# A two-block model on one core: in the first mixer the turns of the input powers, the splits between scan units, the gate's sigmoids and the rows' load change places

## The reference, cut to what matters

```python
def s5_mixer(x, w_in, ..., d_skip, w_glu, b_glu, w_out):
    u, z = jnp.split(x @ w_in, 2, axis=-1)               # 2048 -> 2 x 1024
    ...                                                  # ar, ai: decay; bbar, c: input and output matrices
    _, _, h_r, h_i = lax.associative_scan(...)           # states, 64 groups x 64
    y = einsum(c_re, h_r) - einsum(c_im, h_i) + d_skip * u
    g = jax.nn.gelu(y)
    y = g * jax.nn.sigmoid(g @ w_glu + b_glu)
    return (y * jax.nn.silu(z)) @ w_out                  # 1024 -> 2048
```

## Time and profile before

| | |
|---|---|
| Median of three runs | 3044.75 us |
| Profiled execution, its own time | 3048.8 us |
| Its span in the trace | 3047.0 us |
| Granted clock, mean over the span | 0.991 |
| TensorE busy | 2974.8 us (98%) |
| VectorE busy | 2090.3 us (69%) |
| ScalarE busy | 1713.6 us (56%) |

### The profile page before, as it was taken

The page is one execution under the profiler, slowest core; times in us unless marked ns, Lnnn a source line. Parts: engine busy times, 40 slices in busy tenths (PEclk is TensorE's granted clock), DMA queues, the critical chain, the costliest instruction groups (busy, mean ns, idle before and its releaser), DMA issues.

```text
span 3047.0 us, 57764 instructions
## 1 busy us (share of the span) xinstructions
PE 2974.8 (98%) x23714; PEld 2469.0 (81%) x23714; DVE 2090.3 (69%) x2892; ACT 1713.6 (56%) x2261; POOL 151.1 (5%) x144
## 2 busy tenths in 40 slices
PE   7989999999999899999999999999999999999998
PEld 6868999999998799988999897777777777777654
DVE  7766445555666775756599997777777777777655
ACT  6544344666645533635545794445665656566676
POOL 6000000000000210000000350000000000000000
PEclk9999999999999999999999999999999999999999
DMA  6346565544473433535655426555656666656554
GB/s 231 92 171 211 173 189 177 148 151 147 138 248 114 132 125 113 165 118 182 207 174 189 150 95 220 191 198 189 201 188 199 194 201 194 200 188 206 195 199 152
DMA packets 143961, 529.78 MB, mean 174 GB/s; under 512 B 16992, under 2 KB 17760, under 8 KB 142048
## 3 DMA queue, kind: packets, MB, share of 16 engines
q1 hardware_dynamic: 141120, 515.57, 52.6%
q10 hardware_dynamic: 2592, 10.68, 1.0%
HBM read 521.99 MB, written 4.19 MB: 173 GB/s over the span
## 4 chain that ended last, share of the span: by engine, by line
PE 88%; DVE 6%; ACT 3%; DMA 2%; issue 1%; ACTq 0%; DVEq 0%; SPq 0%
PE ps L309 31%; PE ps L2912 22%; PE ps L2839 22%; DMA mem<-weights 2%; PE ps L451 1%; DVE mem L281 1%; PE ps L942 1%; PE ps L2884 1%; PE ps L1364 1%; PE ps L1991 1%; PE ps L1396 1%; ACT rounded L274 1%; PE ps L344 1%; PE ps L1977 1%; ACT mem L3000 0%
## 5 line engine op out<-in xcount | busy, mean ns | idle before, releaser
L281 DVE TENSOR_TENSOR mem<-mem,rounded 128x1024 bf16<-128x1024 f32 x940 | 1143.2, 1227 | 701.1 <-ACT rounded L274 689.5
L274 ACT CAST rounded<-mem 128x1024 fp32r<-128x1024 f32 x940 | 980.8, 1047 | 915.2 <-PE ps L309 287.4
L309 PE MATMUL ps<-rounded 128*128 128x256 f32 x3168 | 446.7, 290 | 17.5 <-DVE mem L281 17.5
L309 PEld LDWEIGHTS ps<-rounded 128*128 128x128 f32 x3168 | 397.1, 191 | 21.3 <-issue 16.2
L309 PE MATMUL ps<-mem,rounded 128*128 128x256 bf16 x3168 | 403.4, 274 | 1.4 <-DVE mem L281 1.4
L2912 PE MATMUL ps<-rounded 128*128 128x512 f32 x1024 | 337.0, 442 | 2.2 <-DVE mem L3309 2.0
L309 PEld LDWEIGHTS ps<-mem,rounded 128*128 128x128 bf16 x3168 | 302.2, 98 | 43.1 <-DVE mem L281 1.5
L2912 PE MATMUL ps<-mem,rounded 128*128 128x512 bf16 x1024 | 308.2, 383 | 0.0
L3010 ACT CAST mem<-mem 128x1024 bf16<-128x1024 f32 x204 | 213.6, 1047 | 155.5 <-PE ps L2912 68.4
L3299 DVE TENSOR_TENSOR mem<-mem,ps 128x512 f32<-128x512 f32 x384 | 263.1, 685 | 50.6 <-PE ps L2912 33.0
L2839 PE MATMUL ps<-rounded 128*128 128x256 f32 x2048 | 285.7, 287 | 0.5 <-ACT mem L3000 0.4
(11 more groups left out here) (447 smaller groups left out, 2973.7 us busy)
## 6 DMA issues: line engine op xcount, KB each, us to landing
mem<-experts SPq DMA_DIRECT2D x512, 512.0 KB, 4.0
mem<-weights SPq DMA_DIRECT2D x440, 512.0 KB, 3.7
mem<-x_t SPq DMA_DIRECT2D x4, 512.0 KB, 9.8
mem<-x_rows SPq DMA_DIRECT2D x1, 2048.0 KB, 8.4
mem<-cmp_w_k ACTq DMA_DIRECT2D x4, 512.0 KB, 5.0
mem<-cmp_w_v ACTq DMA_DIRECT2D x4, 512.0 KB, 5.2
h_rows<-mem SPq DMA_DIRECT2D x1, 2048.0 KB, 9.7
mem<-h_rows ACTq DMA_DIRECT2D x1, 2048.0 KB, 8.7
```

The costliest lines, as they stand in the source:

```text
L274: self.nc.scalar.copy(self.parts(r % SLOTS)[0], self.raw(r % RAW)).then_inc(self.high_done, with_skipped(c))
L281: self.nc.vector.tensor_tensor(wl, self.raw(r % RAW), wh.bitcast(F32), ALU.subtract).then_inc(self.low_done, with_skipped(c))
L309: mm = self.nc.tensor.matmul(self.ps[:, bank, half * 256:half * 256 + 256], a, b, start=(part == 0 and n == 0), stop=(part == PIECES - 1 a ...
```

## The change

The order changes at five places; no operation is added or dropped.
- TURN_AFTER: the four turns stand behind pieces 13, 16, 19 and 23, before behind 10, 13, 17 and 20. TURNED_AT and EXPAND_AT stay.
- VectorE: three low parts stand between the units (0,1) and (1,0), before four; three behind (1,1), before two. The product of z and the first half of gelu stands ahead of the low part of gelu's second half. Three, and then one, stand behind the two halves of the gated product, before two and two.
- ScalarE: two and three casts stand behind the two halves of gelu, before three and four. One follows the first sigmoids, and two stand before the second, as before.
- SP: pieces 42 and 43 are issued ahead of the rows of x, before behind them.

```diff
--- before.py
+++ after.py
@@ -632,7 +632,7 @@
 S5_GLOW, S5_YLOW, S5_SZ = S5_BT + 4096, S5_BT + 5120, S5_BT + 6144
 
 
-TURN_AFTER = (10, 13, 17, 20)
+TURN_AFTER = (13, 16, 19, 23)
 EXPAND_AT = (13, 15, 20, 24, 25, 27, 29)
 TURNED_AT = (17, 21, 26, 28)
 
@@ -721,7 +721,7 @@
                 sp.dma_start(k.raw(n), ins["weights"][n]).then_inc(k.landed[n], 16)
                 k.issued += 1
         k.stream(sp, AT_GLU, ahead=2 * RAW)
-        k.stream(sp, AT_A_OUT, ahead=2)
+        k.stream(sp, AT_A_OUT, ahead=PIECES)
         sp.wait_ge(h_ready, 4)
         sp.dma_start(rows, ins["x_rows"]).then_inc(xs, 16)
         k.stream(sp, AT_KV, ahead=0)
@@ -841,9 +841,10 @@
                 nc.scalar.activation(dst, src, ACT.Gelu_apprx_tanh).then_inc(gelu_done, 1)
             act.wait_ge(gelu_done, 2 * h + 2)
             nc.scalar.copy(half(gel_parts[0], h), half(gel, h)).then_inc(g_high, 1)
-            more(3 if h == 0 else 4)
+            more(2 if h == 0 else 3)
         for n in range(N_GLU):
-            more(2 * n)
+            if n:
+                more(2)
             t = AT_GLU + n
             act.wait_ge(k.multiplied, G0 + 6 + 2 * n)
             for sub in range(4):
@@ -852,6 +853,8 @@
                                             ps[:, t % BANKS + 3 * (sub // 2), (sub % 2) * T:(sub % 2) * T + T],
                                            ACT.Sigmoid, bias=small[:, 8 + j:9 + j])
                 last.then_inc(k.bank_free if sub == 3 else sig_done, 1)
+            if n == 0:
+                more(1)
             act.wait_ge(y_done, n + 1)
             nc.scalar.copy(half(yy_parts[0], n), half(yy, n)).then_inc(y_high, 1)
             act.dma_start(k.at((LN_G, LN_B)[n], 2048), ins[("ln_g", "ln_b")[n]][0]).then_inc(rows_in, 16)
@@ -1179,24 +1182,24 @@
 
         unit(0, 0)
         unit(0, 1)
-        more(4)
+        more(3)
         unit(1, 0)
         gel_low(0)
         unit(1, 1)
-        more(2)
+        more(3)
+        dve.wait_ge(z_done, 1)
+        v(tt(half(sz, 0), half(sz, 0), half(gel, 0), ALU.mult))
         gel_low(1)
         more(2)
-        dve.wait_ge(z_done, 1)
-        for h in range(2):
-            v(tt(half(sz, h), half(sz, h), half(gel, h), ALU.mult))
-            more(1)
+        v(tt(half(sz, 1), half(sz, 1), half(gel, 1), ALU.mult))
+        more(1)
         for h in range(2):
             dve.wait_ge(sig_done, 3 * h + 3)
             dve.wait_ge(k.bank_free, AT_GLU + h + 1 + BANKS)
             tt(half(yy, h), half(sig, h), half(sz, h), ALU.mult).then_inc(y_done, 1)
             dve.wait_ge(y_high, h + 1)
             tt(half(yy_parts[1], h), half(yy, h), half(yy_parts[0], h).bitcast(F32), ALU.subtract).then_inc(y_low, 1)
-            more(2)
+            more(3 if h == 0 else 1)
         dve.wait_ge(xs, 16)
         for n in range(N_A_OUT - 1):
             t = AT_A_OUT + n
```

## The result

| | median, us | ratio to before, 95% interval | profiled span, us |
|---|---|---|---|
| before | 3045.15 (5 runs) | | 3047.0 |
| changed | 3027.32 (5 runs, 3023.45 to 3033.69) | 0.9943 [0.9927, 0.9958] | 3025.5 |

What follows compares the result with a forecast made beforehand. The prediction took TensorE, 88% of the chain, as the bound, losing time to gaps and cold starts. Terms 12.0 + 3.8 + 8.0 give 23.8 us: 3048.8 profiled becomes 3025.0, or 3021 against the median; range 3017 to 3034.

Steps and rivals of the forecast that it cites:

- Part 1, the turns: Input-power turns on TensorE placed behind later pieces: no new waits, scans start earlier, 12.0 us gained.
- The third copy-out: ScalarE's copy-out before the fourth turn: ends at 85.9, turn at 86.9, the tightest place, clear by 1.0 us.
- The ceiling of 25.5 us: Most any ordering could give in the mixer: TensorE gaps of 18.2 us plus 7.3 us of slow clock.
- Part 2, the splits: Fewer VectorE splits between scan units: the 3.57 us gap before outputs (1,0) goes, 3.8 us gained.
- The wait for unit (1,1): TensorE's wait before outputs (1,1): grows from 0.69 to 2.0 us.
- Part 3, the sigmoids: Sigmoids ahead of casts on ScalarE: the 6.74 us wait and cold start before the output tiles go, 8.0 us gained.
- the table load: Sigmoid table load on ScalarE, 1.28 us: runs in the pause without a wait; if it waits, gain 22.5 us.
- Part 4, the rows' load: 2 MB load on SP's queue issued behind pieces 42 and 43: costs nothing, range 0 to about 4 us.
- main case: Whole kernel at 3019 to 3026 us, chance 0.64.
- rival A: Late landings starve three tight hand-overs, one gap again brings a cold start: gain 14 to 18, 3029 us, chance 0.17.
- a clock drop behind the wait for unit (1,1): Outputs (1,1) on TensorE might take 5.20 instead of 3.73 us, gain then 22.3 us; held 3 in 10.
- Rival D: Turns drain TensorE's stock of pieces, four times 8, 32 us lost against 23.8 gained: 3053 us, chance 0.04.

Runs made afterwards that it cites:

- run 11: Changed kernel with the fourth turn behind piece 21 instead of 23: median 3026.91 us, ratio 0.9942.
- run 12: Changed kernel with the four turns behind pieces 16, 19, 22 and 25: median 3037.43 us, ratio 0.9974.
- run 8: Changed kernel with four splits between units (0,1) and (1,0) and two behind (1,1), as before the change: 3027.39 us, ratio 0.9939.
- run 1: The changed kernel a second time, no edit: median 3025.16 us, ratio 0.9929.
- run 6: Changed kernel with casts 41 and 42 ahead of the first sigmoids, one ahead of the second, rows' load ahead of piece 42 again: 3034.04 us, ratio 0.9963.
- run 5: Changed kernel with casts 41 and 42 ahead of the first sigmoids, one cast ahead of the second: 3027.05 us, ratio 0.9938.
- run 7: Changed kernel with only the rows' load put back ahead of piece 42: 3025.56 us, ratio 0.9934.
- run 9: Changed kernel with two splits behind each gated half instead of three and one: 3023.18 us, ratio 0.9928.
- run 10: Changed kernel with two splits behind each gated half and the convolution's kernel products behind piece 28, not ahead of the first sums: 3021.43 us, ratio 0.9918.
- run 4: Changed kernel with two casts ahead of each of the two sigmoids: median 3037.71 us, ratio 0.9964.
- run 2: Kernel before with only the turns moved, behind pieces 13, 16, 19 and 23: median 3037.19 us, ratio 0.9968.

## Why the prediction was right

- **Part 1, the turns, 12.0 us.** Right. Undone alone they cost 9.7 (23.4 less 13.7), made alone they give 11.2. The third copy-out ended at 86.1 where 85.9 was worked out. The room ahead of the fourth turn was larger than the 1.0 us of the prediction, since the turn needs only the first copy: about 2.4 us, an estimate (87.18 less 84.05 and the 0.73 of run 11). Runs 11 and 12 show both sides of the place: the fourth turn two pieces earlier loses 3.4 us, all four three pieces later 13.9.
- **The ceiling of 25.5 us** was low by about 1.2: it counted the slow clock on the two turns and not on the pieces behind them (49.36 to 62.18 is 12.8 us, where a turn and three pieces take 10.0; from the fourth turn to the kernels 22.7, where 20.9 would do). Its two turn gaps with their cold starts make only 10.6, and its own steps gave 12.0.
- **Part 2, the splits, 3.8 us.** Right in place. Run 8 loses 4.8 us at the mixer's end, 1.6 of it by a clock drop, and that drop stood one wait later than forecast. The wait for unit (1,1) is 1.1 us (run 1), not 2.0.
- **Part 3, the sigmoids, 8.0 us: the sum right, its owner wrong.** With both edits undone the loss is 7.3 us (run 6), or 8.1 counted from outputs (1,1). The step that before "they stood behind casts 41 and 42, the latter waiting 5.34 us for its transfer" took that transfer as given. It was so late because of the rows' load, which the same change moves. With the load behind piece 43 the casts ahead of the sigmoids cost 2.4 us (run 5), the table load and a clock drop included.
- **Part 4, the rows' load, nothing.** Right beside part 3 (run 7: -0.4 us), wrong as the term of a sum: without part 3 it is worth 4.9 (run 5 against 6), or 5.7 counted from outputs (1,1). Each edit covers for the other, and the last 2.4 us need part 3.
- **The total.** The new order alone makes 23.4 us at the mixer's end, 23.8 were forecast. The first profile had 20.9, since a halt and a stretch at half clock cost 2.5 us there; the medians gained 17.8 and 22.5 in two sets of five runs. The first, 3027.3, lies outside the main case (3019 to 3026), and by its size 17.8 would fit rival A; but TensorE has no wait in the profile for the late landings that A rests on, and run 1, with full clock there, has the 23.4. The range had this spread in it, but the prediction had not named its cause: it looked for a clock drop behind the wait for unit (1,1), and none was there (0.82 us). The table load never waited for the semaphore. Not undone alone were the number of casts behind the two halves of gelu and the place of the product of z; three and one low parts behind the gated halves, in place of two and two, made the wait of 1.2 us (run 9).
- **Rival D's price** was too high, as far as run 12 shows, where TensorE twice ran out of pieces behind a turn. ScalarE's stall reaches the end once, through the tables, and not once per turn through TensorE: 13.9 us, not 32.

## What to carry to other kernels

When a wait is for a transfer, ask what stood before that transfer in its queue, and whether the same change moves it, before the wait is booked to the instruction that suffered it. Two edits that remove one wait are priced by undoing each and both. A helper engine that alternates between work for the main stream and waits on the main engine passes its stall on along its own queue, so follow that queue to the next thing that everybody needs.

## What the runs showed of the hardware

- TensorE's issue halted for 0.25 to 2.12 us in all profiles, in the long rows of small matmuls (256 in 7.37 us, 29 ns each): mostly after 120 of the first sums or 11 before the end of outputs (0,1). The same program had it at the one place in one execution and at the other in the next. By count of matmuls the two places are the 985th and the 1750th of the execution, and so they are in run 10, where the 128 matmuls of the kernels stand behind the sums and the halt comes after 248 of them instead of 120. So the place belongs to TensorE's stream of instructions, not to these matmuls (run 4 had its second halt elsewhere, at the 1623rd). No semaphore releases it; but all sixteen halts end 2.2 to 2.6 us after a packet starts on DMA queue q8, which the page calls "instruction" (104.91 and 107.29 us in the changed kernel). That TensorE waits there for its instructions fits this; no run tried it.
- The clock fell to 1.2 GHz behind a halt of only 0.89 us (changed kernel) and 0.64 us (run 4) in the first sums, and not behind the halts in outputs (0,1), which reached 2.12 us (run 12). Of the waits it fell behind those of 3.1 us and more and behind 2.17 (run 8), 2.30 (run 12), 2.43 (run 5) and 2.54 us (run 4), not behind 1.87 (run 7), 2.01 (run 8) nor 2.92 us (run 11). The length of the idle time alone does not decide it; what does stays open. The Trainium skill (TensorE: Matmul & The Clock Gate, What's actually happening) has the throttled clock as the default and activity as what lifts it. The busy time in the trace of the changed kernel does not account for the fall by that: the clock went to 0.50 in a stretch that TensorE was busy throughout, 108 to 112 us, 2 us after a halt of 0.89.
- The clock's losses far behind the mixer vary by execution. From the mixer's end on, TensorE was at half clock for 24 to 28 us in the four profiles with least of it (runs 1, 2, 8, 11), where that part took 2795.8 to 2796.6 us, and for 45 and 47 us in the two with most (runs 4 and 7), where it took 2801.4 and 2802.0. So the clock accounts for much of the spread. Run 1, then run 7, two stretches of the same work:

```profile
900.00:950.00 50.00, 44.79 (x350) 43.03 (x348) 36.10 (x57) 30.41 (x44) 0.00 (x0) 0.86 0.21 66
1000.00:1050.00 50.00, 40.33 (x327) 37.23 (x326) 35.33 (x37) 23.64 (x34) 9.15 (x9) 0.93 0.41 134
```

```profile
900.00:950.00 50.00, 44.79 (x339) 42.39 (x337) 36.13 (x57) 30.14 (x44) 0.00 (x0) 0.83 0.21 64
1000.00:1050.00 50.00, 42.31 (x320) 38.63 (x319) 32.84 (x36) 21.16 (x30) 7.40 (x7) 0.86 0.43 137
```

Run 7 ended the mixer 0.4 us ahead of run 1 and the span 5.7 us behind it.
